# Later loads, two copies for the head sums, and packed sample halves in a one-core encoder layer

## The reference

```python
h = x @ w_in                       # q | k | v | u, 512 columns each, D_MODEL = 1024
z = q k^T / 8                      # 8 heads of 64, keys strictly before the query
a = exp(log_sigmoid(z) + sum over later keys of log(1 - sigmoid(z)))   # stick breaking
A = a @ v
B = ((trailing mean of u over 2, 4, 8, 16) - u) @ pool_w * pool_scale  # 4 groups of 128
x1 = LayerNorm(ALPHA * x + concat[A, B] @ w_out)
y  = LayerNorm(ALPHA * x1 + (silu(x1 @ w_gate) * (x1 @ w_up)) @ w_down)   # D_FF = 2816
```

## Time and profile before

| | |
|---|---|
| median of 3 runs | 2817.24 us (2815.66 to 2817.45) |
| profiled execution | 2819.01 us, span 2817.2 us |
| mean granted TensorE clock | 0.974 |
| PE busy | 2656.3 us (94%), 14586 matmuls |
| PEld busy | 2272.3 us (81%) |
| DVE / ACT / POOL busy | 1534.0 (54%) / 1093.5 (39%) / 1073.5 us (38%) |
| DMA | 373.97 MB, mean 133 GB/s |

### The profile page before, as it was taken

One profiled execution on the slowest core, in us unless ns is written; L12 is line 12 of the kernel. 1 busy time (PEld: TensorE's weight loads), 2 busy tenths in 40 slices (PEclk: granted clock), 3 DMA queues, 4 the chain that ended last, 5 costly groups with the idle time before them and its releaser, 6 DMA issues.

```text
span 2817.2 us, 38701 instructions
## 1 busy us (share of the span) xinstructions
PE 2656.3 (94%) x14586; PEld 2272.3 (81%) x14586; DVE 1534.0 (54%) x2098; ACT 1093.5 (39%) x1868; POOL 1073.5 (38%) x949
## 2 busy tenths in 40 slices
PE   8988898998899999999999999999999998999997
PEld 8966797787677897877778878778877897999996
DVE  4466444777332436677764357777766345433335
ACT  3344324565221224565542245554554213222222
POOL 2344224565231215556442155464553213422222
PEclk9999999999996999999999999999999999999999
DMA  6686865674343624434425243344422612322221
GB/s 193 184 234 192 268 198 180 191 232 126 97 131 97 197 73 133 117 118 131 131 72 191 81 133 108 101 130 134 116 86 80 190 61 90 108 80 90 83 83 70
DMA packets 458183, 373.97 MB, mean 133 GB/s; under 512 B 29447, under 2 KB 391295, under 8 KB 457998
## 3 DMA queue, kind: packets, MB, share of 16 engines
q1 hardware_dynamic: 457998, 371.50, 43.6%
HBM read 303.33 MB, written 68.09 MB: 132 GB/s over the span
## 4 chain that ended last, share of the span: by engine, by line
PE 81%; DVE 6%; issue 5%; DMA 3%; ACT 3%; POOL 2%; SPq 1%; DVEq 0%; ACTq 0%; POOLq 0%
PE bank L1193 33%; PE bank L1209 17%; PE bank L1107 10%; PE bank L1047 7%; PE bank L970 4%; PE bank L1014 4%; PE bank L986 3%; DVE left L1592 2%; DMA gw_lo_raw<-in_w_in_dram 1%; ACT bank L1291 1%; ACT beta L1290 1%; DVE acc L1685 1%; PE bank L1006 1%; POOL acc L1990 1%; DMA k_st<-kcT_scratch 1%
## 5 line engine op out<-in xcount | busy, mean ns | idle before, releaser
L1193 PE MATMUL bank<-x1T,gw_hi 128*128 128x512 f32 (+1 forms) x3520 | 950.5, 359 | 2.6 <-issue 2.5
L1193 PEld LDWEIGHTS bank<-x1T,gw_hi 128*128 128x128 f32 x3520 | 611.3, 190 | 84.4 <-issue 3.1
L1193 PE MATMUL bank<-x1T,gw_lo 128*128 128x512 f32 (+1 forms) x1760 | 624.7, 355 | 0.0
L1983 POOL TENSOR_TENSOR beta<-beta,left 128x512 f32<-128x512 f32 (+2 forms) x326 | 359.3, 1102 | 478.8 <-DVE left L1592 478.0
L1999 POOL TENSOR_TENSOR gw_lo<-gw_lo_raw,gw_hi 128x1024 fp32r<-128x1024 f32 x88 | 213.6, 2427 | 580.2 <-ACT gw_hi L1338 580.2
L1592 DVE TENSOR_TENSOR_SCAN left<-bank,left,zero_t 128x512 f32<-128x512 f32 (+2 forms) x326 | 364.2, 1117 | 99.7 <-ACT bank L1291 84.5
L1107 PE MATMUL bank<-x1T,gw_hi 128*128 128x256 f32 (+2 forms) x1472 | 367.8, 342 | 26.9 <-POOL gw_lo L2012 24.3
L1281 ACT ACTIVATE aT<-bank 128x512 fp32r<-128x512 f32 (+2 forms) x326 | 173.6, 533 | 558.6 <-PE bank L986 521.3
L1193 PEld LDWEIGHTS bank<-x1T,gw_lo 128*128 128x128 f32 x1760 | 334.3, 190 | 48.9
L1583 DVE TENSOR_TENSOR aT<-bank,aT 128x512 fp32r<-128x512 f32 (+2 forms) x326 | 197.5, 606 | 263.4 <-ACT aT L1281 262.3
L1685 DVE TENSOR_TENSOR acc<-bank,acc 128x512 f32<-128x512 f32 x320 | 216.5, 685 | 228.2 <-PE bank L1209 228.0
(11 more groups left out here) (163 smaller groups left out, 3796.5 us busy)
## 6 DMA issues: line engine op xcount, KB each, us to landing
gw_lo_raw<-in_w_gate_dram SPq DMA_DIRECT2D x88, 512.0 KB, 3.9
gw_lo_raw<-in_w_up_dram SPq DMA_DIRECT2D x88, 512.0 KB, 4.0
dw_lo_raw<-in_w_down_dram SPq DMA_DIRECT2D x88, 512.0 KB, 4.4
gw_lo_raw<-in_w_in_dram SPq DMA_DIRECT2D x64, 512.0 KB, 4.8
k_st<-kT_scratch SPq DMA_DIRECT2D x160, 128.0 KB, 2.9
v_st<-v_scratch SPq DMA_DIRECT2D x80, 256.0 KB, 3.6
acc<-in_x_prompt_dram SPq DMA_DIRECT2D x32, 512.0 KB, 6.1
q_st<-qT_scratch SPq DMA_DIRECT2D x128, 128.0 KB, 3.1
```

The source lines that it names most:

```text
L1193: m = pe.matmul(gu_bank(g, n)[:, 0:w], gw[L % 4][a][:, k, :], x1T[x][:, k, first:first + w], start=k == 0 and s == 0, stop=k == KD - 1 and ...
L1983: pool.tensor_tensor(x[:, 0:w], x[:, 0:w], left[n % RL][:, 1:w + 1], ALU.mult).then_inc(a_done, 1)
```

## The change

It has four parts.

1. `step_of` no longer loads a slot of the prompt as soon as it is free: the load's step is the later of that and six steps before its use. The sample's loads keep their steps, but a query load of the sample is 4 DMAs in place of 16.
2. The head sum leaves PSUM by two copies: ACT copies partitions 64 to 127 to `o_t`, at the front of its step, DVE copies partitions 0 to 63 to `o_top`. DVE then adds the two in SBUF. PE's next group waits for the two copies and no longer for the sum.
3. Mixing has 14 steps of loads. It starts three slots later and ends at the same slot. Block 0's x tiles are issued at steps 4 to 7, the norm rows at step 14.
4. The sample's low halves stand in 32 columns of their own beside its high halves (`mixT[0]`, and `hT_hi` for all pairs but the last). Of its three products two remain, with the low half's result in 32 other output rows. `fold` and `add_fold` add these rows, once behind the mixing and once before the last pair's sums. `hidden_lo` becomes two instructions in these pairs. The sample moves to rows 64 to 95 of `acc_s`.

```diff
+    SAMPLE_ROWS, SAMPLE_COLS = slice(P - 2 * DEC, P - DEC), slice(XW + DEC - P, XW + DEC)
+    LOW_ROWS, LOW_COLS = slice(P - DEC, P), slice(XW, XW + DEC)
...
-    LEAD, PIECES = 10, 10
+    LEAD, PIECES = 14, 10
...
-        spread([(MIX, b, s) for s in range(M_STEPS[b])], M_FROM[b], M_FROM[b] + (60 if b == 0 else 84))
+        spread([(MIX, b, s) for s in range(M_STEPS[b])], M_FROM[b] + 3, M_FROM[b] + (60 if b == 0 else 84))
...
-                        for h in range(4):
-                            at0 = h * P + h * DEC
-                            row = (ld.head + h) * HD
-                            sp.dma_start(r32(slot[s, x, at0:at0 + DEC]), r32(qT_d[j, row:row + HD, SEQ:TOK]))\
-                              .then_inc(q_loaded[ld.slot], 16)
+                        to = r32(slot[s, x, 0:DEC])
+                        to = bass.AP(to.tensor, to.offset, [to.ap[0], [P + DEC, 4], [1, DEC]])
+                        row = ld.head * HD
+                        sp.dma_start(to, r32(qT_d[j, row:row + 4 * HD, SEQ:TOK]).rearrange("(h d) t -> d h t", h=4))\
+                          .then_inc(q_loaded[ld.slot], 16)
...
+            def step_of(ld, lag, wanted):
+
+                free = 0
+                if ld.freed_by is not None:
+                    free = ld.freed_by + lag - (ld.parts_before is not None)
+                g = segment_of(wanted)
+                return max(0, free - SEGMENTS[g][0], wanted + lag - 1 - AHEAD - SEGMENTS[g][0])
+
+            AHEAD = 6
...
-                if m == 0 and b == 0:
+                if b == 0 and 4 <= m < 4 + BT:
                     sp.wait_ge(x_turned, x_before(3))
-                    load_x(0)
+                    load_x(0, [m - 4])
                 if m == 0:
                     groups = max(it.group for it in ITEMS if it.block == b) + 1
                     sp.wait_ge(o_stored, 16 * o_issues[groups])
+                if m == LEAD:
                     load_parameters(1, b)
...
                 if opens_group(u) and it.group:
-                    pe.wait_ge(o_sum, it.group)
+                    pe.wait_ge(o_low, it.group)
+                    pe.wait_ge(o_high, it.group)
...
+                products = ((0, 0), (0, 1), (1, 0))
+                if t == BT:
+                    products = ((0, 0), (0, 1)) if p < PAIRS - 1 else ((0, 0), (1, 0), (0, 1))
...
+                u = lo + s - AT_V - 1
+                if lo <= u < hi and closes_group(u):
+                    og, w = ITEMS[u].group, P if ITEMS[u].sample else BW
+                    act.wait_ge(av_done, u + 1)
+                    if og:
+                        act.wait_ge(o_stored, 16 * o_issues[og])
+                    act.activation(o_t[:, 0:w], bank[O_BANK][HD:P, 0:w], ACT.Copy).then_inc(o_low, 1)
...
-                    dve.tensor_copy(o_t[:, 0:w], bank[O_BANK][HD:P, 0:w]).then_inc(o_moved, 1)
-                    dve.wait_ge(o_moved, og + 1)
-                    dve.tensor_tensor(o_t[:, 0:w], bank[O_BANK][0:HD, 0:w], o_t[:, 0:w], ALU.add)\
-                       .then_inc(o_sum, 1)
+                    dve.tensor_copy(o_top[:, 0:w], bank[O_BANK][0:HD, 0:w]).then_inc(o_high, 1)
+                    dve.wait_ge(o_high, og + 1)
+                    dve.wait_ge(o_low, og + 1)
+                    dve.tensor_tensor(o_t[:, 0:w], o_top[:, 0:w], o_t[:, 0:w], ALU.add).then_inc(o_sum, 1)
...
+            def fold(done):
+                dve.tensor_copy(low[SAMPLE_ROWS, :], acc_s[LOW_ROWS, :]).then_inc(folded, 1)
+                dve.wait_ge(folded, done + 1)
+
+            def add_fold(done):
+                dve.tensor_tensor(acc_s[SAMPLE_ROWS, :], acc_s[SAMPLE_ROWS, :], low[SAMPLE_ROWS, :], ALU.add).then_inc(folded, 1)
+                dve.wait_ge(folded, done + 2)
...
+                if packed:
+                    m = dve.tensor_tensor(hT[e][0][:, LOW_COLS], hT[e][2][:, BW:XW], r32(hT[e][0][:, BW:XW]), ALU.subtract)
```

66 lines of the change are left out of this document (43 added, 23 removed).

## The result

| | before | after |
|---|---|---|
| median of 4 runs each | 2817.34 us | 2793.97 us (2792.55 to 2794.85) |
| ratio | | 0.9924, 95% interval 0.991 to 0.9939 |
| profiled execution, span | 2819.01, 2817.2 us | 2792.55, 2790.8 us |
| mean granted clock | 0.974 | 0.978 |
| matmuls | 14586 | 14514 |

A forecast was written before the change was run, and what follows sets the result against it. TensorE was taken as the bound (81% of the chain). Terms 13.1 + 13.4 + 8.1 + 4.5 + 6.5 + 10.1 - 3 = 52.7 us off 2819.0, and 1.8 less for the median: about 2765 us, range 2738 to 2798.

The forecast's parts named there:

- Fewer matmuls: Sample's tile in block 3: 40 matmuls fewer in the feed-forward part, 9.3 us, and 32 in mixing, 3.8: 13.1 us gained.
- PE is not handed back to DVE: Block 3's feed-forward part: DVE idles 0.69 us before the sample's addition, so PE would not come to wait for DVE.
- The fold: Block 3's mixing: an added copy, addition and memset on DVE, some 2.7 us; cost 3 us, between 0 and 8.
- Segment 0: Its start: 12 DMAs in place of 23, weights 7.0 us earlier, 1.1 for the clock: 8.1 us gained.
- Segment 1: Its start: 8 DMAs remain in SP's burst, weights asked for 8.5 us earlier, both stalls shortened: 13.4 us gained with the clock.
- The second stall: Start of segment 1: a 2.45 us stall that follows the same load burst and should go, less 0.3.
- Mixing of block 0: The 9.21 us weight stall shrinks to 4 as x tiles and norm rows go later: 4.5 us gained net.
- the later weight loads now meet the x tiles: Block 0's mixing: a deduction of 1.7 us because x tiles are issued at later steps.
- Sample queries: Second sample group: 4 query DMAs in place of 16 remove a 5.50 us stall; with the clock 6.5 us gained.
- Two copies: Head closings: PE released up to 0.72 us earlier at 18 waits, less 3.3 us of costs: net 10.1 us, between -8 and 15.
- A: Rival: load bursts' gains real, closings' not, as DVE or ACT becomes the bound in attention: 2785 us, chance 0.22.
- C: Rival: weight loads held by something else; only matmuls, sample and half the copies gain: 2795 us, chance 0.08.

The follow-up runs named there:

- u_mix: The changed kernel with part 3 undone (ten mixing load steps, start three slots earlier, x tiles and norm rows at step 0): 2787.86 us, ratio 0.9893.
- n_fold: The changed kernel without the copy and addition behind block 3's mixing, its memset cut to 8 of 1024 columns: 2789.38 us, ratio 0.99.
- p_packed: The kernel before with part 4 alone, both folds included: 2805.98 us, ratio 0.9964.
- n_affine: The changed kernel with GpSimd adding the first LayerNorm's bias to 8 of 1024 columns only, waits kept: 2791.65 us, ratio 0.991.
- p_q4: The kernel before with one edit, a query load of the sample as 4 DMAs in place of 16: 2810.73 us, ratio 0.9979.
- p_ahead: The kernel before with part 1 alone, prompt loads six steps ahead, the sample's queries still 16 DMAs: 2800.59 us, ratio 0.9949.
- p_copies: The kernel before with part 2 alone, the head sum by ACT's copy and DVE's copy and sum: 2808.35 us, ratio 0.9973.
- n_sum: The changed kernel with the sum of the two copies over 8 of 512 columns only, copies and waits kept: 2791.73 us, ratio 0.9916.

## Why the prediction was right and wrong

Set against the forecast place by place, three terms are missing in the changed kernel: the closings of blocks 0 and 1 (10.1 us forecast, 1.1 and 2.9 lost in the two profiles), block 0's mixing (4.5 forecast, 3.5 lost) and the start of segment 1 (13.4 forecast, 5.9 and 5.8 gained). In each the step that failed is of one kind: a load or a copy was moved, and what then stood next in line was put at nothing or nearly so.

**Fewer matmuls: right in kind, 1.4 us too much.** Forecast 9.3 us in the feed-forward part, measured 0.79 us for each of 10 pairs, 7.9 us, in every kernel that has it (7.1 where one pair kept an old gap). The four matmuls did leave at 0.23 us each. But in about one place a pair a matmul now starts 0.34 us after its neighbour in place of 0.23 (5 such between 2480 and 2700 us, none before). The step that said "PE is not handed back to DVE" was nearly right, by 0.14 us a pair.

**The fold: cost mis-sized.** Taken at 3 us, and its instructions sum to 2.8. But it lies in one piece between additions that PE needs, with the statistics next to it, and a low clock follows. From 936 to 2391 us part 4 alone loses 3.4 us and u_mix 1.2, where the mixing's 32 matmuls should give 3.8: a cost of 5 to 7 us, inside the bound of 8 that was given. The fold itself is 3.9 of it (n_fold), and the rest is not followed up. That part 4 as a whole came out as forecast (10.1 and 10.1) is luck. Both of its errors go the same way, and in its own places p_packed gives 7.1 less 3.4, that is 3.7 us. The rest of its gain lies in the stretches that it does not touch.

**Segment 0: right.** 8.1 forecast, 8.1 to 9.2 in all profiles with part 1. The clock's share cannot be told from the rest.

**Segment 1: the step that failed is that the next thing behind SP was nothing.** 13.4 forecast. Part 1 alone gives 10.1, u_mix 11.8, the changed kernel 5.9. The forecast asked of SP when the weights would be requested and not what stood ahead of their subtraction on POOL. With part 3 three bias additions do, 3.2 us of the loss (n_affine). The rest of the wait, 2.92 us, is the load itself: asked for at 434.82 in n_affine, rounded from 441.35 on, with PE there at 441.98. The second stall, 2.45 us, was read as the burst's and was mostly POOL's already.

**Mixing of block 0: wrong sign.** 4.5 gained forecast, 3.5 lost (0.7 gained without part 3). The weights did better than the term: it left 4 us of stall and 1.7 for "the later weight loads now meet the x tiles", and 3.10 us are there. The step that failed is that mixing's own loads were not followed: the last mixT piece is asked for 3.0 us ahead of PE where it was 8.0, and PE waits 4.71 us for it and 2.62 for a transpose's input. And the shift by three slots, taken as free, is what put the bias additions into segment 1's start.

**Sample queries: right alone, not in company.** p_q4 takes 6.5 us at the stall of 5.50 us, exactly the term, and the stall is gone in the changed kernel too. But three key loads behind it are late there:

```profile
722.40 1.22 PE L982 MATMUL bank<-k_st,q_st 128*128 128x512 f32 x2 [2.17 <-DMA k_st<-kcT_scratch]
...
743.94 0.33 PE L982 MATMUL bank<-k_st,q_st 128*128 128x128 f32 x1 [2.35 <-DMA k_st<-kT_scratch]
...
767.39 0.80 PE L982 MATMUL bank<-k_st,q_st 128*128 128x512 f32 x1 [5.92 <-DMA k_st<-kcT_scratch]
```

In the kernel before they were 1.07, 1.81 and 5.05 us. It is not the queries' edit that makes them late: from 731 to 800 us p_q4 has -0.4, and p_ahead and p_copies, which do not touch the sample's loads, lose 3.6 and 5.4 us. So parts 1 and 2 each carry a cost here that the forecast did not have, 5.0 and 6.3 us in the changed kernel. By what way, no run shows.

**Two copies: mis-sized, and the reason given was not the cause.** Net 10.1 forecast, 7.6 alone, 3 in the whole. That the SBUF sum is long in the mean was right (985 ns, 956 forecast), though the mean is of two kinds of sums, as the last section shows, and the loss given to it was too large: n_sum gets nothing back that can be told from scatter. The step that failed is that the head's stores were not followed. The text did name the wait ("ACT too waits for the last store of the previous head") among four things in one term of 3.3 us, and took the store's landing as it was. The move of the loads was not checked against each thing it was moved past: the stores stand in the same SP steps, and at the second closing of block 0 alone this costs 3.36 us.

**Part sums.** The forecast added terms of which two, segment 1 and part 3, exclude each other in part, and two, part 1 and the closings, share a queue. Of the rivals A (bursts real, closings not: 2785) was nearest in its picture of block 0's closings, but its engine was wrong: not DVE or ACT as such, but what they wait for. C (2795) had the size by luck: its weights are held, in part by POOL, but its list of what is gained (matmuls, sample, half of the copies) leaves out segment 0, which is the largest gain.

The signs that the prediction named came out thus: block 3 without gaps in the feed-forward part, yes; 8 DMAs at segment 1, yes; weight waits of 8 us, no (14.0); the second sample group's first key load without a wait, yes (the 2.17 us are at a later one); closing waits 14, no (19.0); clock 0.98, nearly (0.978); and of the signs of being wrong, a prompt key load is among PE's waits once with 0.69 us (0.57 before), ACT's new copy once with 0.4 us, and block 3's mixing stays below "new gaps of more than 5 us": 1.93, 4.13 and 4.03 us in place of 1.64, 0.84 and 2.53.
